# A two-layer encoder trunk in fp32: six places for attention probabilities, value products two outputs behind, and other places for expert weights

## The chip, the cores and the metric
The kernel runs on one core of a Trainium2 chip. The metric is the device time of the whole program in microseconds (us), the median of several executions. PE is TensorE, DVE is VectorE, ACT is ScalarE, POOL is GpSimd, and SP is the engine that issues most of the DMAs.

## The reference, cut to what matters
For 512 tokens of width 1024, each of two layers computes

    mod = SiLU(c) @ W_ada + b_ada                # shifts, scales and gates
    h   = RMSNorm(x) * (1 + scale1) + shift1
    cols = h @ W_in                              # columns of four head groups a, b, c, d
    x   = x + gate1 * (concat(a, b, c, d) @ W_out)
    h   = RMSNorm(x) * (1 + scale2) + shift2
    x   = x + gate2 * HierMoE(h)                 # top group, then top 2 of its 8 experts

and a final RMSNorm follows. Group a is latent attention (4 heads over all 512 keys). Group b is attention within +-128 tokens with a learned sink term. Group c is differential attention: `(softmax(q1 k1) - lam * softmax(q2 k2)) @ v`, so it has two maps for each output, and an RMSNorm per head. Group d is a long convolution by Fourier products. There are 32 experts of hidden width 256 in each layer: `(silu(x @ wg) * (x @ wu)) @ wd`. The three matrices of one expert are 3 MB.

## The kernel before, in words
**Order.** Every engine runs a hand-written list of instructions in program order and waits on semaphores. In each layer the convolution group and the projections come first, then attention, then the output projection, the router and the experts. Layer 0's experts also carry small jobs that prepare layer 1's convolution filters.

**Attention.** `outs` (L358 to L370) has 48 outputs of 128 queries and one head: outputs 0 to 15 are group a, 16 to 31 are group c (the third group of the reference, second in the order), 32 to 47 are group b. `maps` has 64 score maps: 0 to 15 of a, 16 to 47 of c (two for each output), 48 to 63 of b. The planner at L384 to L400 writes one list of steps, and PE, ACT and DVE each run through that same list, doing their own part of a step:
- S (scores of a map): PE makes the product (L753 to L761). For groups a and c, DVE takes the row maximum (L1924) and ACT the exponential (L1404), which writes the map's place in `prob`. For group b, DVE adds the mask and writes the place itself (L1918), takes the maximum (L1919) and its negative (L1921), and ACT takes the exponential in place (L1399, L1400).
- K (group c only): DVE combines the two maps of an output (L1931, L1933, L1935).
- T: PE transposes an output's probabilities (L773) into a PSUM bank, and ACT copies them to a place in `probT` (L1412).
- PV: PE multiplies `probT` by the values (line 495, a helper), and DVE scales the result into `mix_tok` (L1948 or L1944 and L1945, then L1951). At output 31 DVE adds the squares for group c's norm (L1897, L1899), three outputs later it applies the norm (L1904, L1907).
- P and M: PE and ACT make a slice of the modulation (P, all layers), DVE adds it in (M, L1703). They are put in after the outputs named in `MOD_AFTER`.

The step list is K(o), then S up to two maps past the output's own last map, then T(o), then PV(o-1), then M and P where they are due. There are four places in `prob`, so an exponential of map n first waits for the transpose of the output that used map n-4 (L1393); there are two places in `probT`, so the copy of T(n) waits for PV(n-2). Products in PSUM are handed on in two groups of four banks, one for ACT's readers and one for DVE's.

**Experts.** In program order expert e is PE: gate and up product (32 matmuls), transposes of the next expert's tokens, transposes of the activation, down product (8 matmuls). POOL gathers the tokens of expert e+4 and scatter-adds the results of expert e by indirect DMA; SP streams weights. Weights stand in six slots of 3 MB: slots 0 to 3 are in `big`, slot 4 is in the attention arena, slot 5 is in `x_tok` and `mod`. EXPERT_SLOT (L425) uses 2, 3, 0, 1, 4, 5 for the first six experts and then 2, 3, 0, 1 in turn, in both layers. SP loads an expert's gate and up weights after the gate and up product of the expert before it in the slot, and its down weights after the down product (L1144 to L1148); `y_done` counts down products.

**Overfull experts.** An expert takes 64 tokens in its normal turn. What is over goes in extra blocks after expert 31. SP loads a block's weights into OVER_SLOT, which is slot 3, after the last expert in that slot, and that is expert 31 (L1182 to L1185). In these inputs layer 0 has no extra block and layer 1 has one. Behind this same wait SP has, in layer 0, the loads of layer 1's first projection chunk (L1190, after the last expert in slot 1) and of the Fourier matrices (L1192, slot 2). At the end SP waits for all scatters, reads the rows of x back (L1218), and in layer 1 the final norm and the stores follow.

The few lines that set the places and the order:

    prob, probT = at(pr_r, 0, 4, S), at(pr_r, 2048, 2, S)          # L187
    while given < min(v[3][-1] + 3, len(maps)):                    # L389
    EXPERT_SLOT = [2, 3, 0, 1, 4, 5] + [(2, 3, 0, 1)[i % 4] for i in range(NE - 6)]
    sp.wait_ge(y_done, NE * l + last_in_slot(OVER_SLOT[l]) + 1)    # L1182

## Time and profile before

| what | value |
|---|---|
| median of 3 runs | 1601.35 us (1600.17 to 1603.58) |
| profiled execution, its own time | 1594.81 us |
| its span, first to last instruction | 1593.0 us |
| PE busy | 1338.2 us (84% of the span) |
| DVE, ACT, POOL busy | 617.1, 364.6, 268.8 us |
| chain that ended last, by engine | PE 70%, DVE 12%, ACT 7%, issue 5%, DMA 4% |
| DMA | 336.76 MB, 211 GB/s in the mean |
| mean granted clock of PE | 0.948 |

Busy time is an average over stages with different limits. The span divides into layer 0 (0 to 795 us) and layer 1 (to the end); attention is at 268 to 426 us and at 1035 to 1189 us, the experts are at 524 to 794 us and at 1287 to 1549 us. "Issue" is time in which an engine waited for nothing that the profile shows.

### The profile page before, as it was taken

The page shows a single profiled execution, that of the slowest core. Times are in us where ns is not written, and L with a number is a line of the kernel's source. Part 1 is how long each engine was busy: PE and PEld are TensorE (multiplying, and loading weights), DVE is VectorE, ACT ScalarE, POOL GpSimd, SP SyncE. Part 2 cuts the span into 40 slices and gives each one's busy share as a digit, 9 for nine tenths or more (in the row PEclk, how much of TensorE's full clock was granted, in tenths as well). Part 3 has the DMA queues.
Part 4 walks back from the last instruction along what each step waited for, and adds up shares of the span by engine and source line. Part 5 has one row for each costly group of instructions (what it writes and reads, how often), then busy time and mean ns, then how long its engine had stood idle before and what let it go on. Part 6 is the DMA issues. An engine that isn't in the chain of part 4 may idle for free.

```text
span 1593.0 us, 18145 instructions
## 1 busy us (share of the span) xinstructions
PE 1338.2 (84%) x6748; PEld 759.2 (48%) x6748; DVE 617.1 (39%) x1442; ACT 364.6 (23%) x825; POOL 268.8 (17%) x248
## 2 busy tenths in 40 slices
PE   5899999987895798889969999998779769987862
PEld 1446556645542454444434665664454345544441
DVE  4734433477624222432262343246762432211111
ACT  1311024454401111112111202254440211110101
POOL 0201200000000343323210120000000125332321
PEclk8999999999997899999968999999999879999995
DMA  8810222645457599999651122143116668999954
GB/s 299 290 35 19 96 79 80 237 160 154 168 185 316 205 330 378 411 402 408 219 218 40 53 96 79 62 177 132 54 48 226 264 233 313 402 403 406 398 198 183
DMA packets 98609, 336.76 MB, mean 211 GB/s; under 512 B 28370, under 2 KB 33106, under 8 KB 73272
## 3 DMA queue, kind: packets, MB, share of 16 engines
q1 hardware_dynamic: 74712, 305.52, 49.3%
q0 software_dynamic: 15072, 16.85, 4.7%
q10 hardware_dynamic: 8736, 13.21, 2.4%
q8 instruction: 56, 0.92, 0.2%
q14 instruction: 33, 0.27, 0.0%
HBM read 324.08 MB, written 28.98 MB: 222 GB/s over the span
## 4 chain that ended last, share of the span: by engine, by line
PE 70%; DVE 12%; ACT 7%; issue 5%; DMA 4%; POOL 1%; SPq 1%; ACTq 0%; DVEq 0%; POOLq 0%
PE bank L495 65%; DMA big<-in_moe_w_down_dram 2%; PE bank L773 2%; ACT pr_r L1404 2%; PE bank L870 2%; DVE pr_r L2067 2%; ACT pr_r L1451 1%; DVE pr_r L1935 1%; DVE pr_r L2070 1%; DMA big<-in_ada_w_dram 1%; PE bank L610 1%; DVE pr_r L1720 1%; DVE big L1676 1%; DVE small L1919 1%; DVE pr_r L1918 1%
## 5 line engine op out<-in xcount | busy, mean ns | idle before, releaser
L495 PE MATMUL bank<-big,pr_r 128*64 128x256 f32 (+2 forms) x3192 | 453.1, 403 | 88.4 <-issue 26.4
L495 PEld LDWEIGHTS bank<-big,pr_r 128*64 128x64 f32 (+1 forms) x3192 | 273.5, 152 | 239.9 <-issue 113.4
L495 PE MATMUL bank<-big,ht_r 128*128 128x512 f32 (+3 forms) x832 | 308.0, 555 | 1.9 <-ACT ht_r L1417 1.9
L495 PEld LDWEIGHTS bank<-big,ht_r 128*128 128x128 f32 (+1 forms) x832 | 143.8, 189 | 137.3 <-issue 126.0
L495 PE MATMUL bank<-big 128*128 128x256 f32 (+4 forms) x496 | 168.9, 478 | 18.5 <-DVE big L1860 5.7
L1591 POOL DMA_INDIRECT x_rows<-ht_r,slot_i x64 | 102.0, 1593 | 326.0 <-DVE ht_r L2073 312.4
L2067 DVE TENSOR_TENSOR pr_r<-pr_r,bank 64x256 f32<-64x256 f32 x65 | 27.5, 423 | 256.2 <-ACT pr_r L1451 238.4
L495 PEld LDWEIGHTS bank<-big 128*128 128x128 f32 (+2 forms) x496 | 91.6, 197 | 61.5 <-issue 29.7
L1451 ACT ACTIVATE pr_r<-bank 64x256 f32<-64x256 f32 x64 | 24.1, 377 | 410.8 <-PE bank L495 410.8
L1527 POOL TENSOR_SCALAR small<-small 128x1 f32<-128x1 f32 (+2 forms) x20 | 10.1, 504 | 598.2 <-DVE small L1899 336.5
L2073 DVE SCALAR_TENSOR_TENSOR ht_r<-bank,mix_r,mod 128x512 f32<-128x512 f32 x65 | 48.8, 751 | 132.6 <-PE bank L495 132.6
L1404 ACT ACTIVATE pr_r<-bank,small 128x512 f32<-128x512 f32 x96 | 65.4, 684 | 94.9 <-DVE small L1924 49.3
L495 PE MATMUL bank<-ht_r,big 128*128 128x512 f32 x192 | 85.2, 606 | 1.4 <-ACT ht_r L1303 1.4
L1924 DVE TENSOR_REDUCE small<-bank 128x1 f32<-128x512 f32 x96 | 63.3, 685 | 53.0 <-PE bank L495 52.2
L1582 POOL DMA_INDIRECT ht_r<-h_rows,slot_i x64 | 67.9, 1061 | 87.2 <-DVE slot_i L2045 68.4
L773 PE MATMUL bank<-ident,pr_r 128*128 128x128 f32 x336 | 55.4, 282 | 25.7 <-DVE pr_r L1935 24.4
L773 PEld LDWEIGHTS bank<-ident,pr_r 128*128 128x128 f32 x336 | 40.3, 142 | 76.3 <-DVE pr_r L1935 45.7
L495 PEld LDWEIGHTS bank<-ht_r,big 128*128 128x128 f32 x192 | 37.2, 195 | 48.3 <-issue 46.1
L1442 ACT ACTIVATE pr_r<-bank 128x512 f32<-128x512 f32 x65 | 38.8, 597 | 58.7 <-PE bank L856 58.7
L495 PE MATMUL bank<-big,c_rep 128*32 128x256 f32 (+1 forms) x512 | 51.3, 533 | 0.7 <-DMA big<-in_ada_w_dram 0.7
L1412 ACT ACTIVATE pr_r<-bank 128x512 f32<-128x512 f32 (+2 forms) x96 | 50.9, 532 | 1.7 <-PE bank L773 1.7
L856 PE MATMUL bank<-ident,ht_r 128*128 128x128 f32 x260 | 49.3, 313 | 1.8 <-DMA ht_r<-h_rows,slot_i 1.8
(298 smaller groups left out, 1215.0 us busy)
## 6 DMA issues: line engine op xcount, KB each, us to landing
big<-in_moe_w_gate_dram SPq DMA_DIRECT2D x63, 1024.0 KB, 14.7
big<-in_moe_w_up_dram SPq DMA_DIRECT2D x63, 1024.0 KB, 20.9
big<-in_moe_w_down_dram SPq DMA_DIRECT2D x63, 1024.0 KB, 25.5
big<-in_ada_w_dram SPq DMA_DIRECT2D x16, 3072.0 KB, 11.5
big<-in_w_in_dram SPq DMA_DIRECT2D x4, 3072.0 KB, 11.1
big<-in_w_out_dram SPq DMA_DIRECT2D x4, 2048.0 KB, 8.7
mod<-in_ada_b_dram SPq DMA_DIRECT2D x12, 512.0 KB, 10.1
big<-in_w_in_dram SPq DMA_DIRECT2D x2, 2048.0 KB, 8.1
```

The costliest lines, as they stand in the source:

```text
L495: return nc.tensor.matmul(o, l, r, start=start, stop=stop)
L773: last = nc.tensor.transpose(b[:, j * P:(j + 1) * P], prob[:, ms[0] % 4, j * P:(j + 1) * P], ident[:, :])
L856: last = nc.tensor.transpose(bank[b][:, j * P:(j + 1) * P], rows, ident[:, :])
L1404: A_(prob[:, n % 4, :], b[:, :], ACT.Exp, bias=nm[:, n:n + 1], accum_out=rs[:, n:n + 1]).then_inc(taken_a, 1)
L1412: A_(probT[:, n % 2, 0:w], b[:, 0:w], ACT.Copy).then_inc(taken_a, 1)
L1442: return A_(xT[:, b, :], bank[b][:, :], ACT.Copy)
L1451: A_(sil[0:CAP, b, :], bank[2 + b][0:CAP, 0:F], ACT.Silu).then_inc(silu_ready, 1)
L1582: g.indirect_dma_start(out=xg[:, e % 4, :], out_offset=None, in_=half_rows(h2_rows), in_offset=bass.IndirectOffsetOnAxis(ap=slot_i[:, TURN ...
L1591: g.indirect_dma_start(out=half_rows(x_rows), out_offset=bass.IndirectOffsetOnAxis(ap=slot_i[:, TURN[e]:TURN[e] + 1], axis=0), in_=yg[:, e ...
L1924: nc.vector.tensor_reduce(nm[:, n:n + 1], bank[4 + of(f"S{n}")[1] % 4][:, :], X, ALU.max, negate=True).then_inc(nm_ready, 1)
L2067: return TT(act_h[0:CAP, b, :], sil[0:CAP, b, :], bank[2 + b][CAP:P, 0:F], ALU.mult)
L2073: return STT(out=yg[:, b, :], in0=bank[6 + b % 2][:, :], scalar=w, in1=g2, op0=ALU.mult, op1=ALU.mult)
```

## The change
Six edits are made together.
1. `prob` has six places (PB = 6) and moves to `ht_r`, behind group c's queries; `probT` has four places (TB = 4) and takes the freed space.
2. For group c the planner gives scores up to four maps past the output's own (+5 for +3); for a and b it is as before.
3. PV is two outputs behind T (PV(o-2) after T(o)), and the last two follow at the end.
4. Layer 1's experts rotate through all six slots; layer 0's stay.
5. OVER_SLOT is slot 0 in both layers. The last expert in slot 0 is expert 28 in layer 0 and expert 26 in layer 1.
6. The helper functions look up the layer's own slot list.

```diff
-        prob, probT = at(pr_r, 0, 4, S), at(pr_r, 2048, 2, S)
+        PB, TB = 6, 4
+        prob, probT = at(ht_r, 2 * S, PB, S), at(pr_r, 0, TB, S)
...
-                while given < min(v[3][-1] + 3, len(maps)):
+                while given < min(v[3][-1] + (5 if v[0] == "c" else 3), len(maps)):
                     steps.append(("S", given))
                     given += 1
                 steps.append(("T", o))
-                if o:
-                    steps.append(("PV", o - 1))
+                if o >= 2:
+                    steps.append(("PV", o - 2))
...
-            steps.append(("PV", len(outs) - 1))
+            steps += [("PV", len(outs) - 2), ("PV", len(outs) - 1)]
...
-        EXPERT_SLOT = [2, 3, 0, 1, 4, 5] + [(2, 3, 0, 1)[i % 4] for i in range(NE - 6)]
+        SIX = (2, 3, 0, 1, 4, 5)
+        EXPERT_SLOTS = [list(SIX) + [SIX[i % 4] for i in range(NE - 6)], [SIX[i % 6] for i in range(NE)]]
...
-        OVER_SLOT = [3] * DEPTH
+        OVER_SLOT = [0, 0]
...
-                        if n >= 4:
-                            done(act, f"T{out_of[n - 4]}")
+                        if n >= PB:
+                            done(act, f"T{out_of[n - PB]}")
...
-                        if n >= 2:
-                            done(act, f"O{n - 2}")
-                        A_(probT[:, n % 2, 0:w], b[:, 0:w], ACT.Copy).then_inc(taken_a, 1)
+                        if n >= TB:
+                            done(act, f"O{n - TB}")
+                        A_(probT[:, n % TB, 0:w], b[:, 0:w], ACT.Copy).then_inc(taken_a, 1)
...
+                last_in_0 = last_in_slot(0)
                 in_layer[0] = l + 1
...
-                    sp.wait_ge(y_done, NE * l + last_in_slot(0) + 1)
+                    sp.wait_ge(y_done, NE * l + last_in_0 + 1)
```

## Rows read from the trace of the kernel before

**Rows 1.** Windows: busy us of PE, PEld, DVE, ACT, POOL; granted clock, DMA share, GB/s.
```profile
1060.00:1080.00 20.00, 20.00 (x149) 12.08 (x148) 7.80 (x20) 9.32 (x22) 0.00 (x0) 1.00 0.46 161
1141.00:1189.00 48.00, 33.28 (x194) 25.81 (x191) 37.80 (x121) 21.53 (x71) 3.12 (x2) 0.93 0.00 1
```

**Rows 2.** Timeline, layer 1, group c, one round: start, us, engine, line, operation.
```profile
1106.09 0.16 DVE L1931 RECIPROCAL small<-small 128x1 f32<-128x1 f32 x1
...
1107.26 1.28 DVE L1924 TENSOR_REDUCE small<-bank 128x1 f32<-128x512 f32 x2
...
1107.40 0.66 PE L773 MATMUL bank<-ident,pr_r 128*128 128x128 f32 x4 [0.91 <-DVE pr_r L1935]
...
1107.89 1.06 PE L495 MATMUL bank<-big,pr_r 128*128 128x128 f32 x8
1108.06 0.69 ACT L1404 ACTIVATE pr_r<-bank,small 128x512 f32<-128x512 f32 x1 [1.59 <-PE bank L773]
...
1108.99 0.16 DVE L1948 RECIPROCAL small<-small 128x1 f32<-128x1 f32 x1 [0.45 <-PE bank L495]
1109.19 0.28 DVE L1951 TENSOR_SCALAR mix_r<-bank,small 128x64 f32<-128x64 f32 x1
...
1109.61 0.16 DVE L1931 RECIPROCAL small<-small 128x1 f32<-128x1 f32 x1
```

**Rows 3.** Timeline, layer 1, from group c's output 30 to attention's end.
```profile
1141.05 0.16 DVE L1931 RECIPROCAL small<-small 128x1 f32<-128x1 f32 x1
...
1146.79 0.55 DVE L1918 SCALAR_TENSOR_TENSOR pr_r<-bank,mask 128x384 f32<-128x384 f32 x1
...
1148.09 0.15 DVE L1948 RECIPROCAL small<-small 128x1 f32<-128x1 f32 x1
...
1151.41 1.43 DVE L1897 TENSOR_TENSOR big<-mix_r 128x256 f32<-128x256 f32 x4
...
1154.01 0.42 DVE L1918 SCALAR_TENSOR_TENSOR pr_r<-bank,mask 128x256 f32<-128x256 f32 x1
...
1155.04 0.15 DVE L1944 TENSOR_TENSOR small<-small 128x1 f32<-128x1 f32 x1
...
1155.74 0.42 DVE L1918 SCALAR_TENSOR_TENSOR pr_r<-bank,mask 128x256 f32<-128x256 f32 x1
...
1188.42 2.78 PE L799 MATMUL bank<-ident,mix_r 128*128 128x128 f32 x24
```

**Rows 4.** Timeline, between the layers; last row: L1061's time from issue to landing.
```profile
785.10 5.42 PE L495 MATMUL bank<-big,pr_r 128*64 128x512 f32 x40 [0.38 <-DVE pr_r L2070]
...
795.09 0.65 SPq L1061 DMA_DIRECT2D big<-in_k_dft_dram  x1
...
797.92 2.54 PE L495 MATMUL bank<-mix_r,ones 4*128 4x512 f32 x4
...
809.83 16.64 PE L495 MATMUL bank<-x_tok,big 128*128 128x512 f32 x32 [9.36 <-issue]
...
DMA to landing us min/median/max: 14.6/16.4/18.1
```

**Rows 5.** Window (columns as rows 1) and SP's timeline, layer 1's weight stream.
```profile
1336.00:1342.00 6.00, 5.76 (x44) 3.14 (x40) 1.17 (x2) 0.58 (x2) 2.39 (x2) 1.00 0.20 36
...
1341.12 0.33 SPq L1102 DMA_DIRECT2D big<-in_moe_w_gate_dram  x1
```

**Rows 6.** Timeline, expert 31 and the extra block; last row: L1591's landing, layer 1.
```profile
1541.52 3.67 PE L495 MATMUL bank<-big,pr_r 128*64 128x256 f32 x32 [0.91 <-issue]
...
1549.60 0.60 ACT L1442 ACTIVATE pr_r<-bank 128x512 f32<-128x512 f32 x1 [3.99 <-PE bank L856]
...
1560.43 6.47 PE L495 MATMUL bank<-big,pr_r 128*64 128x256 f32 x32 [10.87 <-DMA big<-in_moe_w_down_dram]
...
1572.31 1.55 POOL L1607 DMA_INDIRECT x_rows<-ht_r,over_row_i  x1 [20.20 <-DVE ht_r L2073]
...
DMA to landing us min/median/max: 3.8/8.8/10.1
```

More of the change, by code:

```diff
@@ L431, in trunk @@
                 chunk_at[l, c] = (i, loaded[i])
-            for e, i in enumerate(EXPERT_SLOT):
+            for e, i in enumerate(EXPERT_SLOTS[l]):
                 loaded[i] += 48
@@ L436, in before_in_slot @@
         def before_in_slot(e):
-            return max((n for n in range(e) if EXPERT_SLOT[n] == EXPERT_SLOT[e]), default=None)
+            slots = EXPERT_SLOTS[in_layer[0]]
+            return max((n for n in range(e) if slots[n] == slots[e]), default=None)
         def last_in_slot(s):
-            return max(n for n in range(NE) if EXPERT_SLOT[n] == s)
+            return max(n for n in range(NE) if EXPERT_SLOTS[in_layer[0]][n] == s)
         def chunk_slot(c):
@@ L772, in layer @@
                         for j in range(nb):
-                            last = nc.tensor.transpose(b[:, j * P:(j + 1) * P], prob[:, ms[0] % 4, j * P:(j + 1) * P], ident[:, :])
+                            last = nc.tensor.transpose(b[:, j * P:(j + 1) * P], prob[:, ms[0] % PB, j * P:(j + 1) * P], ident[:, :])
                         last.then_inc(ready_a, 1)
@@ L786, in layer @@
                                  "c": cols_c[:, kt, 512 + h // 2 * P:512 + (h // 2 + 1) * P]}[g]
-                            last = mm(b[:, 0:P], probT[:, n % 2, j * P:(j + 1) * P], v, j == 0, j == len(tiles) - 1)
+                            last = mm(b[:, 0:P], probT[:, n % TB, j * P:(j + 1) * P], v, j == 0, j == len(tiles) - 1)
                         last.then_inc(ready_v, 1)
@@ L881, in expert @@
                 def expert(e):
-                    b, s = e % 2, EXPERT_SLOT[e]
+                    b, s = e % 2, EXPERT_SLOTS[l][e]
                     pe.wait_ge(xt_ready, NE * l + e + 1)
@@ L1098, in load_first @@
                 def load_first(e):
-                    s = EXPERT_SLOT[e]
+                    s = EXPERT_SLOTS[l][e]
                     wg, wu, _ = expert_slot(s)
@@ L1107, in load_down @@
                 def load_down(e):
-                    s = EXPERT_SLOT[e]
+                    s = EXPERT_SLOTS[l][e]
                     src = l * NE + TURN[e]
@@ L1135, in layer @@
                 for e in range(NE):
-                    s = EXPERT_SLOT[e]
+                    s = EXPERT_SLOTS[l][e]
                     if e == 2 and l + 1 < DEPTH:
@@ L1397, in layer @@
                             act.wait_ge(swa_s, 16 * l + n - B_MAPS + 1)
-                            pr = prob[:, n % 4, 0:w]
+                            pr = prob[:, n % PB, 0:w]
                             A_(pr, pr, ACT.Exp, bias=nm[:, n:n + 1], accum_out=rs[:, n:n + 1])
@@ L1403, in layer @@
                             act.wait_ge(nm_ready, 48 * l + n + 1)
-                            A_(prob[:, n % 4, :], b[:, :], ACT.Exp, bias=nm[:, n:n + 1],
+                            A_(prob[:, n % PB, :], b[:, :], ACT.Exp, bias=nm[:, n:n + 1],
                                accum_out=rs[:, n:n + 1]).then_inc(taken_a, 1)
@@ L1915, in layer @@
                             lo, hi = band(qt)
-                            done(v, f"T{out_of[n - 4]}")
-                            pr = prob[:, n % 4, 0:hi - lo]
+                            done(v, f"T{out_of[n - PB]}")
+                            pr = prob[:, n % PB, 0:hi - lo]
                             took(STT(out=pr, in0=b[:, lo:hi], scalar=SWA_SCALE, in1=mask[:, lo:hi], op0=ALU.mult, op1=ALU.add))
@@ L1933, in layer @@
                             step(TS(kap[:, o:o + 1], rs[:, m1_:m1_ + 1], neglam, mx[:, m2_:m2_ + 1], ALU.mult, ALU.mult))
-                            STT(out=prob[:, m1_ % 4, :], in0=prob[:, m2_ % 4, :], scalar=kap[:, o:o + 1],
-                                in1=prob[:, m1_ % 4, :], op0=ALU.mult, op1=ALU.add).then_inc(diff_ready, 1)
+                            STT(out=prob[:, m1_ % PB, :], in0=prob[:, m2_ % PB, :], scalar=kap[:, o:o + 1],
+                                in1=prob[:, m1_ % PB, :], op0=ALU.mult, op1=ALU.add).then_inc(diff_ready, 1)
                     elif what == "PV":
```

## The prediction
> **What bounds the kernel now.** I read the page's chain first, then windows by stage, then the timeline where the change acts, because busy shares mix stages. In group a PE is busy in all of 20 us [rows 1]. From group c's output 30 to attention's end DVE is busy in 37.80 of 48 us and PE in 33.28: nobody is full, so a loop of waits sets the pace [rows 1]. The start and end of such a loop must be read instruction by instruction [rows 2, 3]. Between the layers PE stands still for 9.36 us before the Fourier products, with no releaser shown [rows 4]; its list waits there for the Fourier matrices, issued only at 795.09. In layer 1 the expert weights set the pace from about 1407 us on; early in that stream the DMA engines work only 0.20 of six us, because the next slot comes free at 1341.12 [rows 5]. At the end PE waits 10.87 us for the extra block's weights [rows 6].
>
> **Part 1, group a.** The added places and the later PV move no work, and PE is full there: 0 us. If the later PV left PE without work at the start, one product of 1.06 us [rows 2] would show per layer. I take 0.
>
> **Part 2, group c's round.** A round now takes 1109.61 - 1106.09 = 3.52 us [rows 2]. K starts at 1106.09, the transpose at 1107.40, the exponential at 1108.06: it waited for that transpose to free its place ("1.59 <-PE L773"), and the next K waits for the second exponential. With six places and scores two pairs ahead that wait goes. What is late next? On PE, PV(o-2) still stands behind T(o), which waits for K(o), and DVE evacuates PV(o-2) before K(o+1). That loop is K to transpose 1.31, to the product 0.49, product and hand-over 1.10, to L1951 0.20, its 0.28 and a gap of 0.04: 3.42 us. So only 0.10 us goes, in some 10 undisturbed rounds per layer: 1.0 us. A modulation slice in a round makes PE the bound there as before. A wholly DVE-bound round would be K 1.17 + maxima 1.28 + evacuation 0.52 = 2.97 us; that is the far end, 0.55 us x 10 = 5.5 us per layer.
>
> The first round of c must give four maps rather than two. K 1.17, four maxima 2.56, then PV(14)'s evacuation 0.52 follow in DVE's order, and the transpose waits for an exponential for its bank: about 4.8 us instead of 3.5, so +1.3 us in layer 1. In layer 0 a modulation slice stands just there and I take +1.6.
>
> **Part 3, group b.** From K of output 30 to the transposes of the result is 1188.42 - 1141.05 = 47.4 us in layer 1 [rows 3]. DVE's prices by the starts of its instructions [rows 3]: S with 384 keys 1.30, S with 256 keys 1.03, evacuation of b 0.70, squares 2.60, norm 2 x 1.43 = 2.86; and K 1.17 and evacuation of c 0.52 [rows 2]. After the change this stretch holds 2 K (2.3), 8 + 8 S (18.6), 4 evacuations of c (2.1), squares and norm (5.5) and 12 of b (8.4): 36.9 us. Is DVE kept busy? PV(31) needs the copy of T(31), which stands on ACT behind the exponential of map 51: exponential 0.8, copy 0.6, product 1.06 and hand-overs, less two evacuations that can be done meanwhile: a wait of 1.6 us. After it, PV(o) is wanted two steps (3.9 us) after its S, and its chain needs some 3: no wait. While DVE does the squares, PE and ACT run ahead, which they can't now with PV one behind. The last S leaves exponential, copies and the last value products, 3.5 us (an estimate from 0.69 and 1.06 in rows 2), less the 0.7 of an evacuation already counted. Sum 36.9 + 1.6 + 2.8 = 41.3: **-6.0 us**. Layer 0 has two more modulation slices here; the second falls while DVE does the squares: -5.6. Some of this is work moved to c's start, which I charged there. Attention: layer 1 -6.0 + 1.3 - 1.0 = -5.7, layer 0 -5.6 + 1.6 - 1.0 = -5.0. Bounds for both layers: 0 (the waits only move) and -16 (c's far end, partly).
>
> **Part 4, between the layers.** SP now waits for experts 28, 29 and 30, not 31. The down product of expert 30 ends at 787.04 (785.10 plus its first 8 of 40 matmuls, 1.94 us as elsewhere), and the Fourier load goes out then, 8.0 us sooner than 795.09; the projection chunk ahead of it goes out another expert sooner. PE is through with its modulation products at 800.46 and would start then: **-9.3 us**. The load would have to land within 13.4 us; it took 14.6 in the one case where 3 MB were issued just ahead [rows 4]. That is one bound: landed at 801.7, -8.1. I take -9.3, as the 3 MB will be nearly through. The reads of x wait for Fourier products and all scatters, and shift along.
>
> **Part 5, layer 1's stream.** Expert 10's weights go out after expert 4's product, not after expert 6's, some 14 us sooner. The idle of the engines is 0.80 x 6 = 4.8 us [rows 5]. Afterwards the stream is never starved, so what it gains there arrives at expert 31. I take **-4.4**, as part of the 0.80 is engines finishing earlier than others. The Trainium skill (DMA: Bandwidth & Descriptors, "Why a DMA increments its semaphore by 16 and not by 1") says that only the full count, all engines landed, means that the data is there; by it the 4.8 would overstate the gain, and it would be the slowest engine's idle, under 4.8. The bounds are 2 and 4.8.
>
> **Part 6, the extra block.** Its weights go out behind expert 31's, long before. PE can begin at 1549.60 + 0.60 + 0.1 = 1550.3, against 1560.43: -10.1. The product then runs as expert 31's, 3.67 us, not 6.47 after an idle stretch [rows 6]: -2.8. The weights (3 MB behind expert 31's) must arrive 8.8 us after expert 31's; the stream takes about 9 for an expert: +0.3. **-12.6**. The last scatter waits for expert 31's, which now has less time: landing up to 10.1 us [rows 6] costs up to 1.3. Bounds: -10.3 and -12.9.
>
> **Sum.** -5.7 - 5.0 - 9.3 - 4.4 - 12.6 = -37.0. Against the profiled execution 1594.81 gives 1557.8. The median of the runs is 6.5 us above the profiled one, so 1601.35 - 37.0 = **1564.3**.
>
> **Rivals.** *A: attention gives nothing.* The waits only change name: DVE stays behind PE in b as well, since PE's list is in order. For it speaks c, where I find 0.10 of 3.52. Against it: b's idle DVE is 10 us of 48 [rows 1]. Time 1564 + 11 = 1575.
> *B: attention gives more*, because c's rounds become DVE-bound: 1564 - 6 = 1558. Against it stands the order T(o), PV(o-2) on PE.
> *C: the loads don't gain*: the Fourier load lands late, the stream's slow engine has no idle, the extra weights are late: 1.2 + 2.4 + 2.3 = 6, so 1570.
> *D: slower than before.* With up to two more experts' weights ahead of them, the token gathers and result scatters wait behind the weights. They have a lead of about 3.5 experts, 25 us; they land in 8.8 now [rows 6]. If they queued behind all outstanding weights (up to five times 9 us), each of layer 1's 26 reloaded experts would wait up to 20 us. From a landing of 27 us on (37 / 26 = 1.4 us per expert beyond the lead) the change is slower; at 28 us it is 3 x 26 = 78 - 37 = 41 us slower, 1642. Against it: 8.8 us while 37 us of weights were outstanding says they interleave. The Trainium skill (same page, "Queues, rings and completion order") has each engine take turns between queues at packets, by which D does not occur; the trace agrees with its 8.8 us.
> *E: no extra block moves*, if the profile's 10.87 us were a late token list: 1577. The row names the down weights.
>
> **Chances.** Forecast 0.58, A 0.14, B 0.10, C 0.12, D 0.03, E 0.03. A difference of 0.2% (3.2 us) is about what a measurement of this kernel can tell from none. Faster 0.96, same 0.01, slower 0.03. The range takes in A, B, C and the bounds of the terms: 1554 to 1579; the gains would be 47 and 22 us.
>
> **What would show it.** The Fourier products start within 1 us of the last modulation product; without a gap "<-issue". c's round is 3.42, and exponentials wait no more for L773. From K(30) to L799 41 us, with waits of L1944 for PE gone but for the end. The share of DMA stays above 0.95 from the first reload to the extra block, and its product takes 3.7 us without a wait above 1. Wrong would be: rounds of 3.0 or over 3.5; a first c round above 6; gathers landing above 20 us; a gap of 5 us or more ahead of the extra block.

## The result, and the profile after

The changed kernel takes **1557.62 us** in the median of 4 runs (1556.63 to 1558.7), against 1600.76 us (4 runs, 1595.6 to 1603.58) for the kernel before, run beside it. The ratio is 0.9734, 95% interval 0.9708 to 0.976: 43 us faster. Forecast were 1564.3 us for the median and, against the profiled execution 1594.81, 1557.8 us. The profiled execution after has 1557.26 us (span 1555.4), so from profile to profile the change is -37.55 us, where the sum said -37.0. The median lies 6.7 us below the forecast; where these come from is the main question of the experiments.

Lines of the changed kernel stand 3 or 4 lower than before: scores' maximum L1928, K L1935, value products' evacuation L1952 and L1955, transposes of probabilities L776, exponential L1408, transposes of the result L802.

The busy times and the chain of the page after. PE's work is what it was; the span is shorter around it.

```profile
PE 1332.9 (86%) x6748; PEld 751.9 (48%) x6748; DVE 615.4 (40%) x1442; ACT 364.0 (23%) x825; POOL 268.3 (17%) x248
...
PE 71%; DVE 13%; ACT 6%; issue 5%; DMA 3%; POOL 1%; SPq 0%; ACTq 0%; POOLq 0%; DVEq 0%
```

One round of group c in layer 1, timeline (answers to [rows 2]):

```profile
1097.25 0.16 DVE L1935 RECIPROCAL small<-small 128x1 f32<-128x1 f32 x1
...
1098.43 1.28 DVE L1928 TENSOR_REDUCE small<-bank 128x1 f32<-128x512 f32 x2
...
1098.57 0.65 PE L776 MATMUL bank<-ident,ht_r 128*128 128x128 f32 x4 [0.81 <-DVE ht_r L1939]
1099.06 1.06 PE L498 MATMUL bank<-big,pr_r 128*128 128x128 f32 x8
1099.23 0.69 ACT L1408 ACTIVATE ht_r<-bank,small 128x512 f32<-128x512 f32 x1 [1.49 <-PE bank L776]
...
1100.15 0.16 DVE L1952 RECIPROCAL small<-small 128x1 f32<-128x1 f32 x1 [0.44 <-PE bank L498]
...
1100.67 0.16 DVE L1935 RECIPROCAL small<-small 128x1 f32<-128x1 f32 x1
```

1100.67 - 1097.25 = 3.42 us, as forecast. The first round of c was not as forecast. These are K of output 16, the transpose and product that follow, the evacuation and K of output 17, from the timelines of PE and DVE, and the window that holds the product (columns as in [rows 1]):

```profile
1070.50 0.16 DVE L1935 RECIPROCAL small<-small 128x1 f32<-128x1 f32 x1
...
1073.40 1.02 PE L776 MATMUL bank<-ident,ht_r 128*128 128x128 f32 x4 [1.54 <-ACT ht_r L1408]
1074.21 1.91 PE L498 MATMUL bank<-big,pr_r 128*128 128x128 f32 x8
...
1076.16 0.16 DVE L1952 RECIPROCAL small<-small 128x1 f32<-128x1 f32 x1 [2.00 <-PE bank L498]
...
1076.68 0.16 DVE L1935 RECIPROCAL small<-small 128x1 f32<-128x1 f32 x1
...
1073.40:1076.20 2.80, 2.80 (x14) 2.58 (x14) 0.80 (x3) 2.35 (x7) 0.00 (x0) 0.52 0.15 60
```

It took 6.18 us: PE waited 1.54 us for an exponential, and then worked at a granted clock of 0.52 (that is at 1.2 GHz of 2.4), so that the value product took 1.91 us instead of 1.06.

From K of output 30 to the transposes of the result (answers to [rows 3]), and the window of that stretch:

```profile
1128.09 0.17 DVE L1935 RECIPROCAL small<-small 128x1 f32<-128x1 f32 x1
...
1169.56 0.71 PE L802 MATMUL bank<-ident,mix_r 128*128 128x128 f32 x5
...
1128.09:1169.56 41.47, 31.30 (x191) 23.26 (x189) 35.53 (x118) 20.04 (x67) 3.12 (x2) 0.96 0.00 1
```

41.47 us, forecast 41.3. DVE is busy 86% of it, against 79% before.

Between the layers (answers to [rows 4]): SP's issue of the Fourier matrices, the last modulation product, the Fourier products, and the time from that issue to landing.

```profile
787.25 0.34 SPq L1064 DMA_DIRECT2D big<-in_k_dft_dram  x1
...
798.06 1.45 PE L498 MATMUL bank<-mix_r,ones 4*128 4x512 f32 x4
799.44 15.70 PE L498 MATMUL bank<-x_tok,big 128*128 128x512 f32 x32
...
DMA to landing us min/median/max: 12.1/12.1/12.1
```

The load landed at 787.25 + 12.1 = 799.35 us, and the products begin at 799.44, without a gap, but with nothing to spare.

Layer 1's stream of weights (answers to [rows 5]); after the third expert the engines have no pause any more:

```profile
1290.00:1480.00 190.00, 164.96 (x1148) 93.34 (x1146) 36.63 (x75) 24.26 (x50) 74.34 (x58) 0.99 1.03 400
```

Expert 31 and the extra block, and the landing of layer 1's scatters (answers to [rows 6]):

```profile
1516.65 3.67 PE L498 MATMUL bank<-big,pr_r 128*64 128x256 f32 x32 [1.10 <-issue]
...
1525.46 3.67 PE L498 MATMUL bank<-big,pr_r 128*64 128x256 f32 x32 [0.77 <-ACT pr_r L1446]
...
1534.54 1.55 POOL L1611 DMA_INDIRECT x_rows<-ht_r,over_row_i  x1 [7.31 <-DVE ht_r L2077]
...
DMA to landing us min/median/max: 3.3/8.6/10.3
```

The extra block's product runs as an expert's, with a wait of 0.77 us.

**What the sum missed.** Against the one profile of the kernel before that I had, layer 0's lead from attention was lost again in its experts. This is the timeline after expert 3's gate and up product in layer 0, and a window behind it:

```profile
553.38 1.60 POOL L1595 DMA_INDIRECT x_rows<-ht_r,slot_i  x1 [0.30 <-issue]
553.80 0.74 PE L859 MATMUL bank<-ident,ht_r 128*128 128x128 f32 x4
...
555.28 1.07 POOL L1586 DMA_INDIRECT ht_r<-h_rows,slot_i  x1 [0.30 <-issue]
556.01 0.33 SPq L1105 DMA_DIRECT2D big<-in_moe_w_gate_dram  x1
556.02 0.38 ACT L1455 ACTIVATE pr_r<-bank 64x256 f32<-64x256 f32 x1 [7.99 <-remote]
...
556.90 0.45 PE L873 MATMUL bank<-ident,pr_r 64*128 64x64 f32 x2 [2.36 <-issue]
557.85 7.09 PE L498 MATMUL bank<-big,pr_r 128*64 128x512 f32 x40 [0.50 <-issue]
...
558.00:560.00 2.00, 2.00 (x6) 0.53 (x6) 0.00 (x0) 0.00 (x0) 1.70 (x2) 0.52 0.81 249
```

By its records PE is through with the product before 553.80, but SP and ACT, who both wait for it, go on only at 556.01 and 556.02, over 2 us later. PE then stands for 2.36 us and does the next 40 matmuls in 7.09 us instead of 5.39; the window near their start has a clock of 0.52. I call this the stall. The same stands in layer 1 (2.38 us at 1303.66). The profile of the kernel before has none of it in either layer.

To compare kernels I use four marks: the start of ACT's SiLU of experts 0 and 31 in each layer. The stretch between them is 31 experts long; "0-11" is the part up to expert 11, which at 7.16 us an expert is 78.8 us when nothing stalls.

```
kernel          layer 0: e0    e31   e31-e0  0-11   layer 1: e0     e31    e31-e0  0-11
before            536.2  790.6  254.4   78.8     1298.1  1545.2  247.2   78.8
before_again      536.7  795.1  258.4   82.6     1300.0  1550.9  250.9   83.3
after             532.4  790.7  258.4   82.8     1279.1  1520.4  241.3   83.3
over_only         536.3  797.1  260.8   84.8     1292.8  1543.6  250.8   83.5
rot_only          537.0  797.4  260.4   85.1     1301.4  1542.8  241.4   84.8
attn_only         529.8  789.2  259.4   83.6     1288.3  1540.5  252.2   85.0
table_late        529.4  784.9  255.5   78.8     1273.5  1515.2  241.6   78.8
spread            532.4  786.6  254.3   78.8     1275.7  1516.5  240.8   78.8
rows_two          532.0  786.1  254.1   78.8     1276.1  1518.9  242.7   78.8
c4                528.3  786.7  258.4   82.7     1272.6  1514.0  241.4   82.6
pv1               534.5  792.8  258.3   82.7     1288.6  1530.5  241.8   83.3
c3                529.5  789.7  260.3   84.8     1279.9  1522.1  242.3   82.9
before_spread     538.5  794.9  256.4   78.8     1302.2  1549.0  246.8   78.8
c4_spread         527.4  784.0  256.5   78.8     1271.0  1511.4  240.5   78.8
```

### The profile page after: what moved, and what is told of

Same layout as the page of the kernel before. It is cut to its first block, busy times and chain, and to the rows that moved or that the text cites. A ratio compares the mean times of both kernels' runs of the same rounds, so it can differ in the third digit from the quotient of the medians.

```text
span 1555.4 us, 18139 instructions
## 1 busy us (share of the span) xinstructions
PE 1332.9 (86%) x6748; PEld 751.9 (48%) x6748; DVE 615.4 (40%) x1442; ACT 364.0 (23%) x825; POOL 268.3 (17%) x248
## 4 chain that ended last, share of the span: by engine, by line
PE 71%; DVE 13%; ACT 6%; issue 5%; DMA 3%; POOL 1%; SPq 0%; ACTq 0%; POOLq 0%; DVEq 0%
PE bank L498 65%; PE bank L776 2%; PE bank L873 2%; DMA big<-in_moe_w_down_dram 2%; ACT ht_r L1408 2%; DVE pr_r L2071 1%; DVE ht_r L1939 1%; ACT pr_r L1455 1%; DVE pr_r L2074 1%; DVE ht_r L1922 1%; DVE small L1923 1%; DMA big<-in_ada_w_dram 1%; PE bank L613 1%; PE bank L859 1%; DVE pr_r L1724 1%
## 5 line engine op out<-in xcount | busy, mean ns | idle before, releaser
L498 PE MATMUL bank<-big,pr_r 128*64 128x256 f32 (+2 forms) x3032 | 428.5, 401 | 42.9 <-DVE pr_r L2074 21.1
L498 PEld LDWEIGHTS bank<-big,pr_r 128*64 128x64 f32 (+1 forms) x3032 | 257.1, 152 | 184.5 <-issue 97.0
L1408 ACT ACTIVATE ht_r<-bank,small 128x512 f32<-128x512 f32 x96 | 65.4, 685 | 88.6 <-DVE small L1928 50.0
L776 PE MATMUL bank<-ident,ht_r 128*128 128x128 f32 x336 | 56.6, 286 | 34.2 <-DVE ht_r L1939 21.0
L1928 DVE TENSOR_REDUCE small<-bank 128x1 f32<-128x512 f32 x96 | 63.2, 686 | 54.0 <-PE bank L498 52.8
L776 PEld LDWEIGHTS bank<-ident,ht_r 128*128 128x128 f32 x336 | 38.7, 143 | 87.9 <-DVE ht_r L1939 40.2
L873 PE MATMUL bank<-ident,pr_r 64*128 64x64 f32 x130 | 29.1, 304 | 25.6 <-DVE pr_r L2071 18.8
L859 PE MATMUL bank<-ident,ht_r 128*128 128x128 f32 x260 | 49.3, 313 | 1.4 <-DMA ht_r<-h_rows,slot_i 0.9
```

What stands on the lines that cost most here:

```text
L498: return nc.tensor.matmul(o, l, r, start=start, stop=stop)
L776: last = nc.tensor.transpose(b[:, j * P:(j + 1) * P], prob[:, ms[0] % PB, j * P:(j + 1) * P], ident[:, :])
L859: last = nc.tensor.transpose(bank[b][:, j * P:(j + 1) * P], rows, ident[:, :])
L873: last = nc.tensor.transpose(bank[4 + b][:, j * CAP:(j + 1) * CAP], rows, ident[0:CAP, 0:CAP])
L1408: A_(prob[:, n % PB, :], b[:, :], ACT.Exp, bias=nm[:, n:n + 1], accum_out=rs[:, n:n + 1]).then_inc(taken_a, 1)
L1928: nc.vector.tensor_reduce(nm[:, n:n + 1], bank[4 + of(f"S{n}")[1] % 4][:, :], X, ALU.max, negate=True).then_inc(nm_ready, 1)
```

## The experiments

The kernel before has a median of 1599.53 us beside the first four kernels, 1599.76 beside the next four and 1600.16 beside the last four.

### One part of the change at a time

**over_only**, the kernel before with

```diff
-        OVER_SLOT = [3] * DEPTH
+        OVER_SLOT = [0, 0]
```

> The kernel before with the overfull block's place alone changed (slot 0 in both layers). My theory: the gain between the layers (9.3 us as forecast, 11.6 as the start of layer 1's d projection moved in the trace of the changed kernel) and that of the extra block (12.6 us) are both of this edit alone: together -22 to -25 us, 1577 us median against 1600.8. In its profile the Fourier products follow the modulation products without a gap, and the extra block's gate and up product takes 3.7 us. Rival: the extra block's gain needs the six rotating places as well, since with four places the stream of weights is behind at the end: then only the 9 to 12 us between the layers come, 1589 us, and a wait for DMA of several us stands ahead of the extra block.

Measured: 1578.38 us (4 runs, 1574.65 to 1580.96), ratio 0.9857, interval 0.9821 to 0.9892: -21 us. The Fourier products follow at once, and from expert 31's SiLU in layer 0 to expert 0's in layer 1 it takes 495.6 us instead of 504.9 in the second profile of before: -9.3. From expert 31's SiLU to the extra block's it takes 8.83 us instead of 21.72 [rows 6], and the extra product 3.67 us with a wait of 0.77. The rival falls: this edit needs no rotation.

**rot_only**, the changed kernel with OVER_SLOT, places, lead and value products as before, so that only layer 1's rotation over six slots is left.

> The kernel before with layer 1's six rotating places alone. My theory: -4.4 us (bounds 2 and 4.8), 1596.4 us median, and the time in which experts follow each other every 7.16 us reaches further than expert 15. Rival 1: the engines' idle time of the four-place order is larger than the one window that I read, and the gain is 8 to 10 us (1592), which the trace of the changed kernel suggests (its experts 0 to 31 took 5.1 us less in spite of a stall of 4.5 us). Rival 2: it gives nothing, since the extra block's weights come after the last product anyway.

Measured: 1591.83 us (7 runs, 1587.94 to 1594.36), ratio 0.9948, interval 0.9927 to 0.9969: -7.7 us. Layer 1's experts take 241.4 us, against 247.2 in the first and 250.9 in the second profile of before. Rival 1 was right. In the second profile the hole in the stream is larger than in the one I had read. The windows around expert 10's load, first profile, then second (columns as in [rows 1]):

```profile
1328.00:1338.00 10.00, 8.98 (x62) 4.68 (x63) 2.08 (x5) 1.05 (x3) 4.90 (x4) 1.00 0.83 288
1338.00:1348.00 10.00, 9.36 (x76) 5.42 (x72) 1.89 (x4) 0.97 (x2) 4.19 (x3) 1.00 0.64 220
```

```profile
1330.00:1340.00 10.00, 8.70 (x70) 5.09 (x66) 1.47 (x3) 0.86 (x2) 3.79 (x3) 1.00 0.82 302
1340.00:1350.00 10.00, 8.72 (x60) 4.87 (x58) 2.18 (x5) 1.95 (x4) 3.88 (x4) 1.00 0.30 55
```

Idle in the first is 1.7 + 3.6 = 5.3 us, in the second 1.8 + 7.0 = 8.8. The experts gained 5.8 and 9.5 us against them: the whole idle time of the stream, ramps included, came back at expert 31, and a little more. Against the 1.03 that the unbroken stream shows above, the idle would be 5.9 and 9.4 us. The bytes give another measure: against 400 GB/s the two pairs of windows fall short by 7.3 and 11.1 us. The second hole is larger because of the stall told below: with four slots expert 10's weights wait for expert 6's product, and SP issues them at 1347.56 us instead of 1341.12. Of these 6.4 us the experts' later start is 1.9 and the stall 4.5 (83.3 against 78.8 us up to expert 11).

**attn_only**, the changed kernel with OVER_SLOT and the expert slots as before.

> The kernel before with the three attention edits alone (six and four places, c's scores to +5, value products two behind). Attention itself should be 4.1 us shorter in layer 0 and 5.7 in layer 1, as in the changed kernel's trace. Theory: layer 0's lead is lost again in its experts, to a stall of 2.1 us after expert 3's gate and up product and the half clock after it, because the transfers that begin there come at another moment; layer 1 keeps its 5.7 us only up to the same stall: -2 to -6 us in all, 1595 to 1599. Rival: the stall belongs to the other edits or to chance, and both leads reach the end: -9.8 us, 1591.

Measured: 1591.9 us (10 runs, 1589.23 to 1595.1), ratio 0.9951, interval 0.9937 to 0.9965: -7.6 us, between the two. The stall is there in both layers (experts 0 to 11 take 83.6 and 85.0 us), but layer 0's expert 31 is 5.9 us ahead of the second profile of before: against a kernel that stalls as well, the lead is not lost. The comparison with the one profile without a stall had misled the theory. The measured time lies nearer to the rival's 1591 than to the theory's 1595 to 1599, though the rival's reason, no stall, is not what happened.

The three parts give -21.2, -7.7 and -7.6, together -36.5 us, and all of them at once -42. The intervals (5.7, 3.4 and 2.2 us to each side) are wide enough for that difference; whether anything but noise is in it stays open. By the ratios the parts give -22.9, -8.3 and -7.8, together -39.0, against -42.6 for the whole.

### What the stall is

**before_again**, the kernel before, unchanged.

> The kernel before unchanged, profiled a second time. Its profiled execution of 1594.8 us is below nearly all its other runs (median 1599.5 us of 16), and alone of all profiles has no stall after expert 3. Theory: the stall is usual in this kernel too, so this profile shows experts 3 and 4 of both layers at 9.3 to 11 us instead of 7.16, layer 0's expert 31 some 4 to 6 us later, and a time near 1600; the 6.5 us between the profiled execution and the median, which I took as constant, were this stall. Rival: no stall shows again, the time is about 1595 to 1600, and the offset has another cause.

Measured: 1599.47 us. The stall is there in both layers:

```profile
558.12 0.75 PE L856 MATMUL bank<-ident,ht_r 128*128 128x128 f32 x4
...
560.37 0.33 SPq L1102 DMA_DIRECT2D big<-in_moe_w_gate_dram  x1
560.38 0.38 ACT L1451 ACTIVATE pr_r<-bank 64x256 f32<-64x256 f32 x1 [8.04 <-remote]
```

Experts 0 to 31 take 4.0 us longer in layer 0 and 3.7 in layer 1 than in the first profile. Elsewhere it loses 0.5 us up to layer 0's expert 0, and takes 2.6 us less between the layers' experts and 1.4 less at the extra block, so that 4.7 us are left in all. The theory holds: the prediction was made from an execution without the usual stall.

**table_late**, the changed kernel with

```diff
-                    if e in (1, 2):
-                        table_rows(e - 1)
+                    if e in (12, 14):
+                        table_rows((e - 12) // 2)
```

> The changed kernel with the eight table rows that POOL writes by indirect DMA after experts 1 and 2 put after experts 12 and 14, in both layers. Theory: the stall of PE after expert 3's gate and up product (2.4 us, then 28 to 40 matmuls at half clock, in all 4 us in each layer) comes from POOL's queue of indirect transfers there; without them experts 3 and 4 follow each other every 7.16 us in both layers, layer 0's stream starts 3.8 us sooner, and the time is 4 to 8 us below the changed kernel's 1557.6. Rival: the stall has nothing to do with them; it stays at expert 3, and the time is the same within 1 us (or the stall comes where the rows now are).

Measured: 1552.9 us (4 runs, 1550.86 to 1557.24), ratio to before 0.9713, interval 0.968 to 0.9746: -4.7 us against the changed kernel. Experts 0 to 11 take 78.8 us in both layers, and in layer 1 steps of 10.2 and 9.5 us stand at experts 14 and 16 now, each with a slow one behind it (8.7 and 9.8): in layer 1 the stall went where the rows went. In layer 0 the rows at experts 12 and 14 bring none: the four rows, the scatter and the gather run on POOL from 627.38 to 635.97 us with pauses of 0.3 us and one of 0.64, and ACT sees the product 0.1 us after PE's records have it over:

```profile
633.01 1.59 POOL L1595 DMA_INDIRECT x_rows<-ht_r,slot_i  x1 [0.64 <-issue]
...
635.19 0.75 PE L859 MATMUL bank<-ident,ht_r 128*128 128x128 f32 x4
...
635.29 0.38 ACT L1455 ACTIVATE pr_r<-bank 64x256 f32<-64x256 f32 x1 [6.01 <-issue]
```

Here the scatter behind the rows starts 2.2 us before the product's recorded end; in the rows of the changed kernel above, 0.42 us before it (553.38 and 553.80). In layer 1 the stall costs nothing on the whole (241.6 us for experts 0 to 31, against 241.3), since with six slots the stream sets the end; in layer 0 its absence is worth 2.9 us here, and 4.1 in spread below.

**spread**, the changed kernel with one row at a time:

```diff
-                    if e in (1, 2):
-                        table_rows(e - 1)
+                    if 4 <= e < 12:
+                        table_rows((e - 4) // NT, [(e - 4) % NT])
```

> The changed kernel with the eight table rows one at a time after experts 4 to 11, instead of four in a row after experts 1 and 2. Theory 1: the stall needs the burst (four rows and a scatter back to back, 7 us of POOL); with single rows between scatter and gather no expert from 1 to 11 takes over 7.3 us in either layer, and the time is that with the rows moved late, 1553 us, or 1 us less as layer 1 has no stall at all. Theory 2: each row's transfer can stall PE by itself, wherever it stands; then several experts between 5 and 12 take over 8 us and the time is 1556 or more.

Measured: 1552.16 us (4 runs, 1551.32 to 1555.39), ratio to before 0.9707, interval 0.9691 to 0.9723. No expert up to 11 takes over 7.26 us in either layer. Theory 1's forecast holds; that it is the burst by itself is not shown, since single rows also move the scatter away from the product's end.

**rows_two**, two rows after each of experts 1 to 4.

> The changed kernel with the table rows in pairs after experts 1 to 4. It tells how long a burst the stall needs. If it needs the long burst (four rows, a scatter and a gather, some 8 us without a pause of POOL), experts 1 to 6 follow each other every 7.2 us in both layers and the time is 1552 to 1553. If rows are harmful while the first reloads of weights are under way, however few in a row, the stall of 2 us and the half clock after it show at one or more of experts 2 to 6, and the time is 1556 to 1558.

Measured: no stall in either layer, experts 0 to 31 in 254.1 and 242.7 us; 1556.17 us in 2 runs, where 1552 to 1553 were expected without a stall. Its profile has 1.9 us more in layer 1's experts than spread's; the rest of the miss was not followed up. So rows during the first reloads bring no stall when they come in pairs; four in a row with a scatter behind them do, in eight of the nine profiles that have them here.

**before_spread**, the kernel before with the edit of spread.

> The kernel before with the table rows one at a time after experts 4 to 11, nothing else. Theory: the stall is worth 4.1 us in layer 0 and 3.8 us in layer 1 there (experts 0 to 31 took 258.4 and 250.9 us in the second profile of before, with stalls, and 254.4 and 247.2 in the first, without), so 1599.6 goes to 1592 to 1595 us, the first profile's 1594.8, and the same edit gives about as much before the change as after it. Rival: with four rotating places the stream hides the stall: 1598 or more.

Measured: 1590.64 us (4 runs, 1589.45 to 1596.69), ratio 0.9936, interval 0.992 to 0.9952: -9.5 us, a little more than the 1592 to 1595 us expected. Experts 0 to 11 take 78.8 us in both layers, and layer 1's experts 246.8 us, as in the first profile of before. In layer 0 its profile has 256.4 us for experts 0 to 31, only 2.0 less than the second profile of before, as expert 12 waits longer for its weights. The rival falls.

What follows: without the stall on either side the change is worth 1552.16 - 1590.64 = **-38.5 us**; with it -43.1. The stall costs 9.5 us before and 5.5 after, because the six rotating slots hide it in layer 1 (by the profiles experts 0 to 31 take 3.7 us longer with it there before, and 0.5 as changed).

### Attention, piece by piece

**pv1**, the changed kernel with PV(o-1) after T(o) and the last one alone at the end.

> The changed kernel with value products one output behind again (places and +5 as changed). Theory: the later value products carry group b's gain, so from K of output 30 to the transposes of the result it takes 46 to 47.5 us again in layer 1 (41.5 as changed, 47.4 before), and c's round is longer than 3.42, since the product waits for the copy of its own output on ACT. Rival: the gain of b comes from the six places alone; then this stretch stays at 41 to 43, and the first c round is 1 us shorter as one product less lies ahead.

Measured: 1565.15 us (2 runs). K of output 30 in layer 1, and the transposes of the result, in the timeline:

```profile
1131.53 0.16 DVE L1935 RECIPROCAL small<-small 128x1 f32<-128x1 f32 x1
...
1178.16 2.02 PE L802 MATMUL bank<-ident,mix_r 128*128 128x128 f32 x17
```

46.63 us: group b's gain (5.2 of 5.9 us) is that of the later value products. The remaining 0.7 us is not more than executions differ (47.0 to 48.7 us in the five profiles with the attention order of before and four places). c's round stays 3.42, so the second half of my theory was wrong: in c the value product is not what the lead needs.

**c4**, the changed kernel with `4 if v[0] == "c" else 3`.

> The changed kernel with group c's scores up to three maps past the output's own (+4 for +5). Theory: c's round stays 3.42 us, since its loop K, transpose, product, evacuation has no exponential in it, and the first round of c (6.18 us) has one map's maximum less, 0.64 us: attention 0.6 us shorter in each layer, 147.6 us from the first scores to the transposes of the result in layer 1 against 148.2. Rival: the exponential of the next output's second map comes too late for K again, and the round is 3.5 to 3.7: attention 1 to 3 us longer.

Measured: 1552.2 us (2 runs, 1550.97 and 1553.42), 5.4 below the changed kernel. The round is 3.42; the first round is 3.53 in both layers, not 6.18 less 0.64 = 5.5 as I expected, and the last 3.42, not 4.02. From K of output 16 to K of 30 it takes 54.92 us in layer 1, against 57.59 (2.7 us less), in layer 0 56.77 against 60.07 (3.3 less). Part of this is the clock: in attn_only, where PE keeps 1.00 in the first round, this stretch takes 56.38 and 58.56 us, so that 1.5 and 1.8 us are the order's and 1.2 and 1.5 the low clock's. I had priced one maximum, 0.64 us, and forgot what was waiting behind it. With +5, four score products fill ACT's four banks before the first transpose of c, so the transpose waits 1.54 us for an exponential, and DVE 2.00 us for the value product behind it (rows above). With +4 there are three, and K, the transpose and the evacuation follow without a wait:

```profile
1068.06 0.17 DVE L1935 RECIPROCAL small<-small 128x1 f32<-128x1 f32 x1
...
1069.38 0.66 PE L776 MATMUL bank<-ident,ht_r 128*128 128x128 f32 x4
...
1071.04 0.15 DVE L1952 RECIPROCAL small<-small 128x1 f32<-128x1 f32 x1
```

**c3**, the same with 3, as before.

> The changed kernel with group c's scores up to two maps past the output's own, as before the change (+3), with six places and value products two behind. Theory: K of the next output now waits for the second exponential of the maps just scored: K start to the first maximum's end 1.81 us, then two exponentials and their hand-overs, 3.5 us and a little more; so c's round is 3.5 to 3.6 us and the whole of group c 1 to 2 us longer than with +4, and the time 1553 to 1555. Rival: the places alone broke the loop, the round is 3.42 as with +4, the first round 2.9 to 3.4, and the time 1551 to 1552.

Measured: 1560.74 us (2 runs), 6 us above the 1553 to 1555 expected and 8.5 above c4. By the profiles of the two, 4.1 us of this come between the layers' experts, 3.2 of them between K(16) and K(30) of layer 1, where three late rounds take 3.88, 4.13 and 4.76 us for a reason that was not sought; 1.9 us are a longer stall in layer 0. Two Ks of layer 1 and the exponential between them:

```profile
1074.02 0.16 DVE L1935 RECIPROCAL small<-small 128x1 f32<-128x1 f32 x1
...
1075.20 1.28 DVE L1928 TENSOR_REDUCE small<-bank 128x1 f32<-128x512 f32 x2
...
1076.00 0.69 ACT L1408 ACTIVATE ht_r<-bank,small 128x512 f32<-128x512 f32 x1 [1.59 <-PE bank L776]
...
1077.55 0.16 DVE L1935 RECIPROCAL small<-small 128x1 f32<-128x1 f32 x1
```

The round is 3.53 us again, with six places. Its exponential starts 0.80 us after the start of the maxima and is put down to the transpose; in [rows 2] it starts at 1108.06, 0.80 after 1107.26, and is put down to the transpose too. With six places that transpose frees nothing this exponential needs, and still it starts at the same moment. So its limit was its own maximum. In [rows 2] the transpose ends at 1107.40 + 0.66 = 1108.06, just when the exponential starts, and the first of the two maxima 0.68 us after 1107.26, at 1107.94. The timeline names the later one. But in spread an exponential that it puts down to its maximum starts at 1068.03 for a maximum at 1067.23, again 0.80 us. That the transpose ends just there is chance. The places only make room for the lead; the lead is what counts.

### Both together

**c4_spread**, the edits of c4 and spread.

> The changed kernel with both: c's scores up to +4, and the table rows one at a time after experts 4 to 11. c's first round 3.5 us and its last 3.42 in both layers, no expert from 1 to 11 over 7.3 us. If the two gains (5.4 and 5.4 us against the changed kernel's 1557.6) add up: 1546.8 us. If they overlap, because layer 1's end is set by the stream of weights from expert 20 on and part of c4's gain was of chance ahead of layer 0's experts: 1549 to 1551.

Measured: **1546.76 us** (5 runs, 1546.24 to 1550.69), ratio to before 0.967, interval 0.9653 to 0.9686, so 10.9 us below the changed kernel. The gains add up. It is the best of all kernels here.

## Why the prediction was right, and where it was not

**Part 1, group a: 0.** Right as to work. K of output 16 comes 1.6 us sooner after the first scores in layer 1, since one value product of 1.06 us now comes behind it (in pv1 it does not come sooner); it is paid for in c.

**Part 2, group c.** The round is 3.42 us, as worked out, and the loop from K through transpose, product and evacuation is what sets it. The wait that I said would go, the exponential's for the transposed place, was none: c3 shows that the loop before ran from K through maxima and two exponentials back to K. The first round, forecast 4.8 us, is 4.98 where PE keeps its clock (both layers of attn_only) and 6.18 to 6.25 where it falls to 0.52. By the prediction's own list, a first round above 6 was to be a sign of error, and it was one: I had left out that the clock can be low after PE's wait there. In layer 0 the forecast was +1.6 and the round grew by 2.7 (6.25 against 3.53), and by 1.5 at full clock (4.98). The last round took 4.02 us, 0.6 more, of which there was no word.

**Part 3, group b.** 41.47 us in layer 1, forecast 41.3; 42.61 in layer 0, forecast 47.8 - 5.6 = 42.2. pv1 shows the mechanism.

**Attention in all.** From the first scores to the transposes of the result: layer 1 153.93 to 148.18 us, -5.75 (forecast -5.7); layer 0 157.36 to 153.24, -4.1 (forecast -5.0). Against the second profile of before, where the stretches are 0.8 and 1.1 us longer, the gains are 6.5 and 5.2. Layer 1's sum is right in part by offset: group a is 1.6 us shorter up to K(16), and c cost 1.7 us between K(16) and K(30), of which 1.2 is the low clock of the first round (57.59 against 56.38 us in attn_only).

**Part 4, between the layers.** Forecast -9.3, from the first profile -11.8 by the start of layer 1's d projection (841.25 to 829.62 us, with expert 31's down product at the same time). 9.4 are the gap; the other 2 us are modulation and Fourier products that ran slower before (2.54 and 16.64 us [rows 4], now 1.45 and 15.70). The load had to land within 13.4 us, and took 12.1 in the changed kernel and 12.3 in over_only, less than the 14.6 of [rows 4]; the late landing with its -8.1 did not come. Against the second profile of before (PE's gap there is 10.39 us) the same count gives -10.9.

**Part 5, layer 1's stream.** The term that was mis-sized: -4.4, bounds 2 and 4.8, measured -5.8 and -9.5 against the two profiles of before (rot_only), -6.4 without any stall (spread against before). I took 0.80 x 6 us from one window; with the ramps on both sides the idle is 5.3 us there, and 8.8 in the usual execution. By the Trainium skill (DMA: Bandwidth & Descriptors, "Why a DMA increments its semaphore by 16 and not by 1") I had taken less than the mean idle. No row here speaks for that cut: the gain was the full mean idle and a little more. The step to 9.5 against the usual execution is the stall's, which the one window could not show.

**Part 6, the extra block.** -12.6 forecast; from SiLU to SiLU 21.72 us became 8.82, -12.9.

**The path from the sum to the median.** This is the step that failed: "the median of the runs is 6.5 us above the profiled one", and I carried this offset over as a constant. It was no constant. The stall after expert 3 was absent in that one execution; in the second profile of before, which has it, the offset is gone (1599.47 against a median of 1599.76), and so it is in the changed kernel's profile (1557.26 and 1557.62). Of the stall's 7.7 us in the two layers other stretches of the second profile take back 3.0, so the size of the offset is the stall's only in part. Nor is every offset a stall: the profile of before_spread has none and lies 6 us above its median (1596.69 and 1590.64). That the profile forecast still came out within 0.6 us (1557.8 for 1557.26) is luck, by offsets: layer 0's experts gave back 4.0 us to the stall, and terms 4 and 5 gave 4 us more than forecast. A further 1.5 us went to no term: from the start of layer 1's d projection to its first maximum it takes 194.4 us in the first profile of before and 192.9 as changed; the second profile of before has 191.8, so this is a difference of executions. The stretches add up: -3.8 to layer 0's expert 0, +4.0 in layer 0's experts, -19.1 to layer 1's expert 0, -5.9 in its experts, -12.9 to the extra block and +0.2 at the end, -37.5 in all.

**The rivals.** A (attention gives nothing), C (loads don't gain) and E are out by the rows above. B came in part: attention could give more, but with +4 and not by rounds bound by DVE. D did not occur: the scatters land in 3.3/8.6/10.3 us with more weights outstanding, against 3.8/8.8/10.1 [rows 6]. That the queues take turns (the Trainium skill, DMA: Bandwidth & Descriptors, "Queues, rings and completion order") agrees with this.

## What to carry to other kernels

Give a software pipeline only as much lead as its loop needs: the lead broke one loop here, and one map more than needed cost 1.5 to 1.8 us at the change of groups at full clock, 3 us where the clock fell, because every engine goes through the new head start in order. A name in square brackets is the event that came last by the trace; when another thing that the instruction needs ended within some 0.1 us of it, add up that chain too before you say what an edit removes. And when the profiled execution is faster than nearly all runs, don't take the difference for a constant, as something may be missing in that execution: profile again before you carry it over.

## What the hardware showed

**Behind a burst of indirect transfers PE's signals can come late.** In eight profiles with four row transfers and a scatter back to back on POOL (about 7 us) early in the reloads, SP and ACT see the end of a product over 2 us after PE's records have it over, in both layers; one profile with the same order shows nothing. Rows moved to experts 12 and 14 move the stall in layer 1 and bring none in layer 0, and with at most two rows in a row (four kernels) it is gone. So in these runs there is no stall without the burst, but the burst is not enough. A second condition fits all the stalls, and no run separates it from the burst: in each of the 18 (two in each of nine profiles) the scatter behind the rows starts 0.37 to 0.43 us before the product's recorded end. Of the 850 products without a stall for which it can be read, only the two of the first profile of before have a scatter that close, the others 0.8 us or more; the burst of layer 0 in table_late, the second burst of each layer and all kernels with single rows or pairs do not. So it may be the meeting of that scatter with the product's end that counts, and the rows only because they push the scatter there. Where the 2 us go, inside PE's last matmuls or on the way of the signal, the trace does not tell: the Trainium skill (Perfetto Trace Analysis, "Tensor Engine Instruction (MATMUL, LD_WEIGHTS)") says that PE's end times are estimated from the instruction's size and that the semaphore is sent only when PSUM has acknowledged the writes, so the 553.80 above need not be the true end. Why a burst would hold it up was not settled.

**The same idle time does or does not cost the clock.** Before the first transpose of group c PE waits 1.54 us in the changed kernel and in spread alike. In the first it then works at 0.52, in the second, in the timeline of PE below (layer 1), at full speed:

```profile
1068.95 0.63 PE L776 MATMUL bank<-ident,ht_r 128*128 128x128 f32 x4 [1.54 <-ACT ht_r L1408]
1069.41 1.06 PE L498 MATMUL bank<-big,pr_r 128*128 128x128 f32 x8
```

A wait of that length was worth 1.2 us more in one execution than in the other (a first round of 6.18 against 4.98 us). Six kernels have +5, and of their twelve first rounds, two in each, six took 6.17 to 6.25 us and six 4.97 or 4.98; in spread layer 0 has the one and layer 1 the other. The wait is 1.54 us in all twelve. With +4 (c4, c4_spread) there is none and with +3 (c3) one of 0.82 us, and their six first rounds took 3.52 or 3.53 us.
